# x transposed inside a key unit and value units run inside a projection unit, with the first loads and tables reordered to match

## The reference, cut to what matters

```python
proj = x @ w_in                                   # split into 14 pieces
ret  = retention(rope(r_q), rope(r_k), r_v) * silu(r_z)
s5o  = s5(s_u, ...) * silu(s_z)                   # complex-diagonal scan, its powers from a_re, a_im, log_dt
ml   = head_norm(mlstm(...) * sigmoid(m_o)) * ml_gn * silu(m_z)
mk, mv = split(mem @ xa_w_kv)                     # keys and values of the memory
xa   = memory_attention(a_q, mk, mv) * silu(a_z)
x    = layer_norm(ALPHA * x + concat(ret, s5o, ml, xa) @ w_out)
```

## Time and profile before

| | |
|---|---|
| Median of 3 runs | 2023.06 us (2016.93 to 2025.28) |
| The profiled execution | 2015.21 us |
| Its span, first to last instruction | 2013.3 us |
| Mean granted TensorE clock | 0.971 of full speed |
| TensorE busy (matmuls) | 1869.4 us, 93% |
| VectorE, ScalarE, GpSimd busy | 1066.9, 611.4, 547.5 us |

### The profile page before, as it was taken

One profiled execution on the slowest core, in us unless ns is written; L12 is line 12 of the kernel. 1 busy time (PEld: TensorE's weight loads), 2 busy tenths in 40 slices (PEclk: granted clock), 3 DMA queues, 4 the chain that ended last, 5 costly groups with the idle time before them and its releaser, 6 DMA issues.

```text
span 2013.3 us, 27375 instructions
## 1 busy us (share of the span) xinstructions
PE 1869.4 (93%) x11136; PEld 1625.3 (81%) x11136; DVE 1066.9 (53%) x1998; ACT 611.4 (30%) x866; POOL 547.5 (27%) x250
## 2 busy tenths in 40 slices
PE   3899899999999997989999989999999999979997
PEld 3777698779988896777878777978899879967786
DVE  8387643543365376417784776254613645852434
ACT  3333225433013401333233322444211342132320
POOL 3243302210111313235434322130111121132461
PEclk8999999999999998999999999999999999989999
DMA  6243325313112114474434332541310311057541
GB/s 242 80 144 92 103 79 208 143 64 85 43 46 91 53 48 151 146 284 142 148 118 136 99 109 76 205 167 53 105 43 22 105 64 48 25 202 274 170 147 63
DMA packets 97932, 232.75 MB, mean 116 GB/s; under 512 B 10632, under 2 KB 40664, under 8 KB 96784
## 3 DMA queue, kind: packets, MB, share of 16 engines
q1 hardware_dynamic: 71680, 176.77, 27.1%
q10 hardware_dynamic: 26048, 54.01, 7.3%
q0 software_dynamic: 80, 0.23, 0.0%
HBM read 168.32 MB, written 58.43 MB: 113 GB/s over the span
## 4 chain that ended last, share of the span: by engine, by line
PE 75%; DVE 12%; DMA 5%; ACT 3%; issue 2%; POOL 2%; SPq 1%; ACTq 0%; DVEq 0%
PE gp L534 18%; PE gp L536 17%; PE gp L535 17%; DMA wraw<-in_w 4%; PE mm L534 2%; PE mm L535 2%; PE mm L536 2%; POOL wlo L1023 2%; PE mm L733 1%; PE mm L866 1%; PE mm L641 1%; DVE sz L1765 1%; PE mm L711 1%; ACT whi L1111 1%; DMA yraw<-yt 1%
## 5 line engine op out<-in xcount | busy, mean ns | idle before, releaser
L1023 POOL TENSOR_TENSOR wlo<-wraw,whi 128x1024 fp32r<-128x1024 f32 x172 | 441.1, 2581 | 1217.7 <-ACT whi L1111 1217.4
L534 PE MATMUL gp<-whi,xh 128*128 128x256 f32 x1280 | 384.1, 300 | 0.0
L536 PE MATMUL gp<-whi,xl 128*128 128x256 f32 x1280 | 361.8, 283 | 0.0
L535 PE MATMUL gp<-wlo,xh 128*128 128x256 f32 x1280 | 361.6, 283 | 0.0
L534 PE MATMUL gp<-xh,whi 128*128 128x512 f32 x768 | 324.7, 423 | 5.7 <-issue 3.4
L536 PE MATMUL gp<-xh,wlo 128*128 128x512 f32 x768 | 304.6, 397 | 0.0
L535 PE MATMUL gp<-xl,whi 128*128 128x512 f32 x768 | 304.3, 396 | 0.0
L534 PEld LDWEIGHTS gp<-whi,xh 128*128 128x128 f32 x1280 | 244.5, 191 | 9.9 <-issue 8.6
L1111 ACT ACTIVATE whi<-wraw 128x1024 fp32r<-128x1024 f32 x172 | 175.9, 1054 | 249.8 <-DMA wraw<-in_w 141.4
L535 PEld LDWEIGHTS gp<-wlo,xh 128*128 128x128 f32 x1280 | 244.9, 191 | 5.8 <-issue 5.7
L536 PEld LDWEIGHTS gp<-whi,xl 128*128 128x128 f32 x1280 | 244.3, 191 | 0.0
(11 more groups left out here) (311 smaller groups left out, 3072.6 us busy)
## 6 DMA issues: line engine op xcount, KB each, us to landing
wraw<-in_w SPq DMA_DIRECT2D x172, 512.0 KB, 3.8
spill<-gate ACTq DMA_DIRECT2D x32, 512.0 KB, 2.6
yraw<-yt SPq DMA_DIRECT2D x32, 512.0 KB, 6.0
xs<-xr SPq DMA_DIRECT2D x16, 512.0 KB, 4.2
xr<-in_x ACTq DMA_DIRECT2D x8, 512.0 KB, 7.3
ud<-gate ACTq DMA_DIRECT2D x8, 512.0 KB, 2.6
uu<-ud SPq DMA_DIRECT2D x64, 64.0 KB, 3.5
p_tab<-kd SPq DMA_DIRECT2D x64, 64.0 KB
```

Of the source, the lines that this page charges most:

```text
L534: nc.tensor.matmul(out, ah, bh, start=start, stop=False)
L535: nc.tensor.matmul(out, ah, bl, start=False, stop=False)
L536: return nc.tensor.matmul(out, al, bh, start=False, stop=stop)
L1023: nc.gpsimd.tensor_tensor(wlo[slot(u)][:, 1024 * i:1024 * i + 1024], wraw[n % 2], whi[slot(u)][:, 1024 * i:1024 * i + 1024].bitcast(F32), ...
```

## The change

It does five things.

- The transposes of x stand inside unit `U_MK + 1`, one group of four behind each of its 16 steps of three matmuls.
- The two value units are no longer units of their own. `values_unit(l, i)` writes the banks 0 and 1 of mm in place of gp, and stands inside `U_SU[0]`, behind its steps 5 and 10 (`MVH`). They have their own semaphores `mv_done` and `mv_free`; the counts of `g_done` and `g_free` leave them out (`units_to`). `U_MV + 1` takes weight slot 1, the slot that `U_MV` has and that `U_SU[1]` takes after it.
- In the first layer SyncE issues the loads of x, four behind the first unit's weights and four behind the second's. The load of the positions comes after the transposes, and rp lies where x lay.
- The low parts of the first two units of the program are made on VectorE (`first_lo`). VectorE begins with the first part of `powers`, which has the 32-column work only, then meml, then those low parts. The power table (`power_table`) and the rotation's angles (`rope_angles`) follow behind x's low parts. ScalarE makes the rotation's tables behind the high part of `U_SU[1]`; the S5 tables' first loads (`bc_load`) and `begin_tables` wait for their store (`rope_st`), in the first layer only.
- ScalarE begins with a one-column copy, which takes the first table load with it; in the second layer the third unit's weights are issued one row store earlier.

```diff
+MVH = (5, 10)
+NGU = NUNIT - 2
...
-        rp = at("rp", 4096, o_x + 8192)
+        rp = at("rp", 4096, R[0])
...
+        def units_to(l, u):
+            return NGU * l + (u + 1 if u < U_MV else u - 1)
...
         def slot(u):
+            if u == U_MV + 1:
+                return 1
...
             mem_load()
             raw(0, U_MK)
+            x_load(0)
             raw(0, U_MK + 1)
+            x_load(1)
...
                 if l:
                     sp.wait_ge(S["xs_out"], 128 * l)
+                else:
+                    sp.dma_start(rp[:, 1024:2048].bitcast(I32), bass.AP(dram["pos"].tensor, 0, [[0, 128], [1, T]])).then_inc(S["pos_in"], 16)
+                raw(l, U_MV + 1)
+                raw(l, U_SU[1])
+                if l == 0:
+                    sp.wait_ge(S["rope_st"], 32)
                 bc_load(l, 0)
                 bc_load(l, 1)
...
+            def values_unit(l, i):
+                u = U_MV + i
+                wh, wl = whi[slot(u)], wlo[slot(u)]
+                pe.wait_ge(S["lo_done"], l * HALVES + half0(u) + nhalf(u))
+                for g in range(2):
+                    if i:
+                        pe.wait_ge(S["mv_free"], 4 * l + g + 1)
+                    for k in range(KT):
+                        a0 = NMEM * k + 128 * g
+                        last = mm3(bank[g][:, 0:256], memh[:, a0:a0 + 128], meml[:, a0:a0 + 128],
+                                   wh[:, 256 * k:256 * k + 256], wl[:, 256 * k:256 * k + 256], k == 0, k == KT - 1)
+                    last.then_inc(S["mv_done"], 1)
...
-                unit(l, U_MK + 1)
+                unit(l, U_MK + 1, x_columns)
...
-                unit(l, U_SU[0])
-                unit(l, U_MV)
-                unit(l, U_MV + 1)
+                unit(l, U_SU[0], lambda i: values_unit(l, MVH.index(i)) if i in MVH else None)
...
+                    if i == 3:
+                        split(l, U_SU[0])
+                    if i == 8:
+                        keys_evict(U_MK + 1, 0)
+                keys_evict(U_MK + 1, 1)
...
+                split(l, U_MV)
+                values_evict(0)
+                split(l, U_MV + 1)
+                u_spill(0, 0)
                 act.wait_ge(S["s_pow"], l + 1)
...
+                values_evict(1)
+                split(l, U_SU[1])
...
+                act.dma_start(dram["kvs"], mkv).then_inc(S["kv_out"], 16)
+                if l == 0:
+                    rope_tables()
                 u_spill(0, 1)
...
+            powers(0)
             mem_split(0)
-            powers(0)
+            first_lo(U_MK)
+            first_lo(U_MK + 1)
...
+                if l == 0:
+                    power_table(l)
+                    rope_angles()
                 coefficients(l)
                 if l == 0:
                     dve.wait_ge(S["kd_zeroed"], 16)
+                    dve.wait_ge(S["rope_st"], 32)
                 begin_tables(l, 0)
```

More of the change, by code:

```diff
@@ L518, in _ @@
                     raw(l + 1, U_MK + 1)
[L519 to L520 removed]
+                    rows_out(4)
+                    rows_out(5)
                     raw(l + 1, U_MK + 2)
+                    rows_out(6)
                     rows_out(7)
@@ L1055, in _ @@
             for l in range(DEPTH):
-                for u in range(U_MK, U_SZ):
+                for u in range(U_MK if l else U_SU[0], U_SZ):
                     lo(l, u)
```

145 lines of the change are left out of this document (73 added, 72 removed).

## The result

The changed kernel takes 1994.05 us in the median of 4 runs (1988.12 to 1995.27). The kernel before, on the same chip, takes 2020.67 us (2016.93 to 2025.28). The ratio is 0.9861, with a 95% interval of 0.9831 to 0.9892: faster, by 26.6 us. The forecast was 1995 us, with a range of 1983 to 2008. The profiled execution took 1995.27 us, its span is 1993.3 us and the mean granted clock 0.973; it is 19.9 us shorter than the profiled execution of the kernel before.

A forecast was written before the change was run, and what follows sets the result against it. TensorE is busy 93% of the span, so only its stops can give time: 20.5 us (first layer) plus 7.5 (second) make 28.0 off a profiled 2015.2, 1987.2; against the median, 7.85 higher, 1995 us, range 1983 to 2008.

The forecast's parts named there:

- The likeliest case: Whole kernel: 20.5 us gained in the first layer and 7.5 in the second, median 1995 us; forecast has 0.61.
- passed on to the outputs: First layer's S5 outputs: the tables' lateness of 5.35 us reaches TensorE in full, leaving 20.5 of 25.9 us gain.
- The four terms: First layer: VectorE start without blocks, transpose steps 0.80 us, end wait 1.7, value units at full clock in 33.5 us.
- the sum without a drain: ScalarE's sines of the power table: 2.7 us with table load, to 66.2; the skill's 1.38 us drain left out.
- I take 2.6, since little else moves then: Rotation's two stores, issued by 77.4 us: landing takes 2.6 us, against 10.2 in the crowded start.
- A wait at the first matmul of the S5 outputs of 7 to 8 us: Sign in the first layer: this wait replaces one of 2.40 us, with low clock behind it.
- 1045.0 against 1046.93: Second layer, start of `U_SU[0]`: 1.9 us earlier through transposes inside the second key unit.
- So nothing comes late: Second layer: tables have no rope to wait for and p_co can begin early, so 7.5 us is gained together.
- the tables are free sooner: Rival at the first S5 tables: VectorE's lateness hidden, up to 5.4 us more gained, 1990 us; chance 0.15.
- The rope chain is longer: Rival in the first layer: stores at 10.2 us and missed handoffs lose 8 to 12 us more, 2005; chance 0.15.
- The transposes fit: Rival denied, second key unit: steps wait for xh and xl (1.28 us), 7.7 us more per layer, 2010; chance 0.07.
- ScalarE's queue did not stand: Rival denied: ScalarE's wait for the power table delays `U_SU[1]`'s split, making the kernel slower, 2033 us; chance 0.02.

The follow-up runs named there:

- the two pairs of profiles: Profiled executions of the changed kernel and the kernel before, then both again unchanged: spans 1993.3 against 2013.3, then 1995.7 against 2011.0 us.
- three variants with the new start: Changed kernel with x's transposes back behind the key unit (1999.36 us), rope angles in VectorE's idle stretches (1985.14), or ScalarE's early copy of the key unit (1994.76).
- the stretch without the 3.02 us stop: Changed kernel with ScalarE copying the second layer's first key unit out of PSUM ahead of the last norm: 1994.76 us, ratio 0.9891.

## Why the prediction was right

The likeliest case came about. The steps of the first layer came as they were given, with one wait in another place; those of the second layer did not all. Step by step:

| step | forecast | measured |
|---|---|---|
| first matmul | 17.8 | 17.20 |
| `U_SU[0]`, layer 1 | 40.4 | 40.76 |
| `U_SU[0]` to `U_SU[1]` | 33.5 | 33.87 |
| power table done, sines done | 63.5, 66.2 | 63.5, 66.3 |
| last activation of the rotation ends | 76.8 | 78.51 |
| tables behind `U_SU[1]` | 8.7 | 10.6 |
| passed on to the outputs | 5.4 | 7.2 |
| gain at the first outputs | 20.5 | 18.0 |
| layer 2, to `U_SU[0]` | 1.9 | 0.3 |
| layer 2, `U_SU[0]` to `U_SU[1]` | 5.6 | 5.7 |
| kept to the end | 28.0 | 20.0 and 15.3 |

- **The start and the interleavings** were right within 0.4 us at each place. The four terms (VectorE's start without the blocks, steps of 0.80 us, 1.7 us of end wait, value units at full clock) hold; the only stop in the transposes is 1.02 us, where 0.3 was taken, and the end wait is 1.46.
- **ScalarE's table load.** The load has 1.28 us and the next activation begins at its end, so the sum without a drain was the right one. This goes against the Trainium skill (ScalarE: Activation LUTs, What ACT_TABLE_LOAD costs), whose drain of 1.38 us the trace again does not show:

```profile
63.54 0.45 ACT L1284 ACTIVATE s_cos<-s_ang 128x288 f32<-128x288 f32 x1 [3.81 <-DVE s_ang L1601]
64.00 1.28 ACT L1285 ACT_TABLE_LOAD   x1
65.30 0.54 ACT L1285 ACTIVATE s_cos<-s_cos,cst 128x288 f32<-128x288 f32 x1
75.17 1.06 ACT L1272 ACTIVATE rp<-rp 128x1024 f32<-128x1024 f32 x1 [5.44 <-DVE rp L1601]
```

- **"I take 2.6, since little else moves then"** and the end of the angles are the terms that were too small. VectorE's last two groups of angles took 5.94 and 2.77 us beside GpSimd's subtractions (1.7 us late at the activations), the stores took 3.1 us to land for 2.6, and p_bc 2.5 for 2.3 (the 2.69 in the last row is how long VectorE stood for it):

```profile
66.39 5.94 DVE L1600 SCALAR_TENSOR_TENSOR rp<-rp 128x1024 f32<-128x1024 f32 x3
72.37 2.77 DVE L1601 TENSOR_SCALAR rp<-rp 128x1024 f32<-128x1024 f32 x1
85.22 1.57 DVE L1716 TENSOR_TENSOR p_tab<-p_jr,p_co 128x516 f32<-128x516 f32 x1 [2.69 <-DMA p_bc<-in_s5bc]
```

- **"A wait at the first matmul of the S5 outputs of 7 to 8 us"** was the wrong place. The wait came one step earlier, in the inputs (5.23 us) and with 1.44 us at `U_SZ`; then the lower clock carried TensorE to the outputs with no wait left. That the lateness is passed on, and its size within 2 us, was right.
- **"1045.0 against 1046.93"** failed: 0.3 us in place of 1.9. I had costed the second layer's steps at 0.80 us right behind a stop of 3 us. TensorE ran there at 0.62 of its clock for 4.5 us, 1.7 us lost. The kernel before had run its keys at full clock behind the same stop, so the row that would have warned was not there; the earlier trace rows, with a clock of 0.65 behind a stop, was.
- **"So nothing comes late"** in the second layer held for its tables, not for its end: in the two pairs of profiles 4.5 and 6.3 us were lost in stops and low clock farther on, a term that the sum did not have at all. Some 3.5 of them are the lower clock that three variants with the new start did not show, and 1.0 is the longer wait at the fourth S5 stop.
- **The total.** In profiled terms the forecast was 1987.2 and the execution took 1995.3, 8 us more. Against the median it was off by 1 us, because the profiled execution of before lies 5.5 us below that kernel's new median and that of the changed kernel 1.2 above its own. The gain of the runs is 26.6 us in one comparison and, by 0.9887 with 2016.6, some 22.8 in another; 28 was too much by 1 to 5 us. That the medians met is partly luck.

The rivals: "the tables are free sooner" is refuted by the 5.23 us wait. "The rope chain is longer" is what happened in direction, by 1.9 us, not by 8 to 12. The transposes fit (0.80 us per step, and 1.28 only at the lower clock behind the second layer's stop). ScalarE's queue did not stand: 0.40 us at `U_SU[1]`.

## What to carry to other kernels

An interleaving is worth what its inputs' arrival allows: with the old start the two gave nothing in the first layer and 8 us in the second; with the new one, taking them out lost 4.3 and 6 us at their places, and the start itself was worth 12 us of span. Before work is moved onto VectorE, look which GpSimd instructions run beside its new place. Here VectorE's arithmetic, copies and scans on SBUF alone were held until a GpSimd instruction ended (zc 2.42 us for 0.43), and xl, which reads PSUM, was not (0.69 us). And a gain at the start is not all kept: stops and low clock farther on took back 4.5 and 6.3 us, and one profile of each variant can't tell differences of 5 us apart. Before a loss is put down to a change, look for a variant that has the same stop without it.

## What was not expected of the hardware

- Which of two engines starts first, by as little as 0.02 us, went with over 2 us of waiting 1.1 ms into the program, in all 13 profiles (2.17 to 2.23 us against 4.01 to 4.41). So two executions of one kernel part there with no change in the program.
- The same stop is not always followed by the lower clock: behind 3.01 us the kernel before had 1.00 over the next 4.5 us, the changed one behind 3.02 us had 0.62. Behind 2.23 us the clock over 9.5 us was 1.00 in six profiles and 0.82 in seven.
- Taking away a stop takes away its low clock (clock 1.00 in the stretch without the 3.02 us stop), but the two together gave back 2.5 us of the 4.7 that they had cost, since VectorE was the bound just behind.
